# Output projection ordered by halves of x, with the transposes of x placed between products

## What is computed

```python
def rms_norm(x, g):
    y = x * rsqrt(mean(x * x) + NORM_EPS)
    return y * g
...
    x = x + concat(rms_norm(a, gain_a), rms_norm(b, gain_b), rms_norm(c, gain_c)) @ w_out
    x = x + relu(rms_norm(x, ln2_g) @ w_up) ** 2 @ w_down
```

## Time and profile before

| | us |
|---|---|
| median of 3 runs | 657.12 |
| lowest, highest | 655.36, 657.3 |
| the profiled execution, its own time | 657.18 |
| its span in the trace | 655.4 |
| TensorE busy | 618.9 |
| mean granted TensorE clock | 0.991 |

### The profile page before, as it was taken

One profiled execution on the slowest core, in us unless ns is written; L12 is line 12 of the kernel. 1 busy time (PEld: TensorE's weight loads), 2 busy tenths in 40 slices (PEclk: granted clock), 3 DMA queues, 4 the chain that ended last, 5 costly groups with the idle time before them and its releaser, 6 DMA issues.

```text
span 655.4 us, 11268 instructions
## 1 busy us (share of the span) xinstructions
PE 618.9 (94%) x4268; PEld 533.2 (81%) x4268; DVE 430.0 (66%) x796; ACT 361.6 (55%) x674; POOL 234.6 (36%) x407
## 2 busy tenths in 40 slices
PE   5999988998999999999999999799899999999995
PEld 4868865688998899889878787568798899899984
DVE  7599898476655696774575877846755545554553
ACT  5756588735546434443456657984545544444451
POOL 6899258515045999910004304771000000000001
PEclk9999998999999999999999999999899999999998
DMA  9584604156854557366638640314466566657631
GB/s 266 168 235 121 140 2 114 33 155 202 258 186 151 185 164 254 128 226 193 190 83 262 124 129 2 82 65 128 134 216 196 167 200 190 188 166 217 192 98 65
DMA packets 55440, 102.79 MB, mean 157 GB/s; under 512 B 12713, under 2 KB 18906, under 8 KB 55354
## 3 DMA queue, kind: packets, MB, share of 16 engines
q1 hardware_dynamic: 48986, 96.04, 48.2%
q0 software_dynamic: 1792, 4.07, 2.6%
q10 hardware_dynamic: 4608, 1.97, 1.1%
HBM read 99.69 MB, written 1.31 MB: 154 GB/s over the span
## 4 chain that ended last, share of the span: by engine, by line
PE 73%; DVE 15%; ACT 5%; issue 3%; POOL 2%; DMA 1%; SPq 0%; DVEq 0%; POOLq 0%; ACTq 0%
PE pb L1744 72%; DVE w_lo L1314 5%; DVE x L1242 2%; ACT tab_zone L1114 1%; ACT w_hi L871 1%; DVE dtmp L1235 1%; POOL dtmp L794 1%; DVE sc_zone L1638 1%; ACT ptmp L1127 1%; DMA raw<-in_w_in 1%; DVE dtmp L1514 1%; DVE top L1510 1%; PE pb L1871 1%; PE pb L2135 1%; DVE tab_zone L1235 1%
## 5 line engine op out<-in xcount | busy, mean ns | idle before, releaser
L1314 DVE TENSOR_TENSOR w_lo<-raw,w_hi 128x1024 fp32r<-128x1024 f32 (+2 forms) x176 | 223.6, 1286 | 139.5 <-ACT w_hi L871 138.6
L871 ACT ACTIVATE w_hi<-raw 128x1024 fp32r<-128x1024 f32 (+2 forms) x184 | 187.9, 1028 | 201.3 <-PE pb L1744 178.5
L1744 PE MATMUL pb<-h_hi,w_hi 128*128 128x256 f32 x512 | 146.1, 285 | 2.5 <-DVE h_lo L1242 1.8
L1744 PE MATMUL pb<-h_hi,w_lo 128*128 128x256 f32 x512 | 145.6, 284 | 0.0
L1744 PE MATMUL pb<-h_lo,w_hi 128*128 128x256 f32 x512 | 145.5, 284 | 0.0
L1744 PEld LDWEIGHTS pb<-h_hi,w_hi 128*128 128x128 f32 x512 | 98.9, 193 | 4.1 <-DVE w_lo L1314 3.0
L1744 PE MATMUL pb<-w_hi,z_hi 128*128 128x512 f32 x256 | 100.0, 390 | 0.4 <-DVE w_lo L1314 0.4
L1744 PE MATMUL pb<-w_hi,z_lo 128*128 128x512 f32 x256 | 99.9, 390 | 0.0
L1744 PE MATMUL pb<-w_lo,z_hi 128*128 128x512 f32 x256 | 99.7, 389 | 0.0
L1744 PEld LDWEIGHTS pb<-h_hi,w_lo 128*128 128x128 f32 x512 | 99.0, 193 | 0.4
L1744 PEld LDWEIGHTS pb<-h_lo,w_hi 128*128 128x128 f32 x512 | 98.9, 193 | 0.0
(11 more groups left out here) (309 smaller groups left out, 852.3 us busy)
## 6 DMA issues: line engine op xcount, KB each, us to landing
raw<-in_w_up SPq DMA_DIRECT2D x64, 512.0 KB, 3.7
raw<-in_w_down SPq DMA_DIRECT2D x64, 512.0 KB, 4.2
raw<-in_w_in SPq DMA_DIRECT2D x24, 512.0 KB, 4.9
raw<-in_w_out SPq DMA_DIRECT2D x8, 512.0 KB, 3.7
raw<-in_w_out SPq DMA_DIRECT2D x16, 256.0 KB, 4.1
raw<-in_w_in SPq DMA_DIRECT2D x8, 308.0 KB, 3.2
raw<-in_w_in SPq DMA_DIRECT2D x8, 280.0 KB, 3.0
x<-in_x ACTq DMA_DIRECT2D x4, 256.0 KB, 4.0
```

What stands on the lines that cost most here:

```text
L871: hi_made.by(act.activation(w_hi[:, n % RING, 0:width(n)], raw[:, n % RING, 0:width(n)], ACT.Copy))
L1314: lo_made.by(dve.tensor_tensor(w_lo[:, n % RING, 0:width(n)], raw[:, n % RING, 0:width(n)], w_hi[:, n % RING, 0:width(n)].bitcast(F32), AL ...
L1744: return pe.matmul(o, l, r, start=start, stop=stop, skip_group_check=True)
```

## The change

The order of the output projection becomes half 0 B, C, A, then half 1 B, C, A, on the same cycle of banks. Piece 23 is now half 0 A; pieces 24 to 27 are half 1 B, C, C, A. The two-load pieces (group C) are 21, 22, 25 and 26.

All six sums of squares are done at once behind piece 21 (`block_sums`), which waits for the squares of A too; there is one copy by ScalarE and one `rstd` of six columns.

For the MLP, the eight transposes of the first half of x stand ahead of piece 27 (`transpose_first`), and those of the second half behind the first piece of `w_up` (`transpose_second`), token tile by token tile, in banks 4, 7, 2, 3. The first `w_up` chunk takes its blocks in the order of `UP_ORDER`: 2, 3, 0, 1, 4 to 7. ScalarE makes `h_hi` of 2, 3, waits for piece 27 to be used, makes 0, 1, then `hi` of piece 31, then 4 to 7. VectorE makes `h_lo` of 2, 3 ahead of the last addition, the others behind it, and `lo` of piece 31 behind all of them.

Between the layers, half 1 of the last `w_down` product runs its first piece for both token tiles, then the other three for token tile 0 (`down_t0`), then the eight transposes of the first half of x, then the three pieces for token tile 1. The other eight transposes stand behind the next layer's first `w_in` piece. VectorE makes `lo` of that piece and the first two `h_lo` between its additions.

The diff, cut to its core:

```diff
-TWO_LOADS = (P_IN + 1, P_IN + 2, P_IN + 4, P_IN + 5)
+TWO_LOADS = (P_IN + 1, P_IN + 2, P_IN + 5, P_IN + 6)
...
-        OUT = [(0, 1, (1,), (0, 1)), (0, 2, (2, 3), (2, 3)), (1, 1, (1,), (5, 6)),
-               (1, 2, (2, 3), (0, 1)), (0, 0, (0,), (2, 3)), (1, 0, (0,), (5, 6))]
+        OUT = [(half, g, qs, banks) for half in range(2)
+               for g, qs, banks in ((1, (1,), (0, 1)), (2, (2, 3), (2, 3)), (0, (0,), (5, 6)))]
+        UP_ORDER = (2, 3, 0, 1, 4, 5, 6, 7)
...
-            bank = (0, 1, 2, 3)[k // 2] if stage == 0 else (4, 7, 5, 6)[k // 2]
+            bank = (0, 1, 2, 3)[k // 2] if stage == 0 else (4, 7, 2, 3)[k // 2]
...
-                rstd(L, 3, rg[:, 2:6], stat[:, 6:10], 1.0)
-                rstd(L, 4, rg[:, 0:2], stat[:, 4:6], 1.0)
-                rstd(L, 5, r2[:], stat[:, 10:12], D_MODEL)
+                rstd(L, 3, rg[:], stat[:, 4:10], 1.0)
+                rstd(L, 4, r2[:], stat[:, 10:12], D_MODEL)
...
-                    if L:
+                    if L and n < 2:
                         h_parts(L, 0, g1[:, L], (2 * n, 2 * n + 1))
+                if L:
+                    h_parts(L, 0, g1[:, L], range(4, KB))
...
                 for n in range(24, P_UP0 + 4):
-                    if n in (25, 27):
-                        i = (n - 25) // 2
-                        act.wait_ge(st_ps.sem, st_ps.at(L, i + 1))
-                        a, b = ((6, 10), (4, 6))[i]
-                        sq_sum.by(act.activation(stat[:, a:b], pb[7][:, a:b], ACT.Copy))
+                    if n == 25:
+                        act.wait_ge(st_ps.sem, st_ps.at(L, 1))
+                        sq_sum.by(act.activation(stat[:, 4:10], pb[7][:, 4:10], ACT.Copy))
+                    if n == P_UP0 + 3:
+                        h_parts(L, 2, g2[:, L], (2, 3))
+                        act.wait_ge(used.sem, used.at(L, P_UP0))
+                        h_parts(L, 2, g2[:, L], (0, 1))
                     hi(L, n)
-                h_parts(L, 2, g2[:, L])
+                h_parts(L, 2, g2[:, L], range(4, KB))
                 sums(L, 10, sq_sum.by)
...
-                    for n in ((25,), (26,), (27,), (28, 29), (30,), (31,))[s]:
+                    for n in ((25,), (26,), (27,), (28, 29), (30,), ())[s]:
                         lo(n)
-                h_rest(16, g2[:, L], lambda k: xT_rows(k, 2))
+                    if s == 4:
+                        h_rest(16, g2[:, L], lambda k: xT_rows(k, 2), UP_ORDER, 0, 2)
+                h_rest(16, g2[:, L], lambda k: xT_rows(k, 2), UP_ORDER, 2, 6)
+                lo(31)
...
                         for t in range(TT):
+                            if (half, t) == (1, 0):
+                                dve.wait_ge(down_t0.sem, down_t0.at(L, 1))
+                            if (half, t) == (1, 1):
+                                dve.wait_ge(used.sem, used.at(L, PIECES))
                             dst = x[:, t, half * 512:(half + 1) * 512]
                             x_new.by(stt(dst, pb[4 + 2 * t + half][:], r2[:, t:t + 1], dst, ALU.mult, ALU.add))
+                            if (half, t) == (0, 1):
+                                lo(0, 1)
+                            if (half, t) == (1, 0):
+                                h_rest(0, g1[:, L + 1], lambda k: xT_rows(k, 0), first=0, count=2, ahead=1)
...
+                def transpose_first(lyr, k_new, stage):
+                    pe.wait_ge(x_new.sem, x_new.at(lyr, k_new - 2))
+                    for k in range(4):
+                        for t in range(TT):
+                            m = x_turned(k, t, stage)
+                        if k % 2:
+                            xT_ps.by(m)
+                def transpose_second(k_new, stage):
+                    for t in range(TT):
+                        pe.wait_ge(x_new.sem, x_new.at(L, k_new - 1 + t))
+                        for k in range(4, KB):
+                            m = x_turned(k, t, stage)
+                            if k % 2 and t:
+                                xT_ps.by(m)
...
-                    pe.wait_ge(h_lo_made.sem, h_lo_made.at(L, (10, 14, 14, 14, 16, 16)[s]))
+                    pe.wait_ge(h_lo_made.sem, h_lo_made.at(L, (10, 14, 16, 16, 16, 16)[s]))
+                    if s == 5:
+                        transpose_first(L, 8, 2)
                     for q in qs:
                         out_piece(n, half, q, banks, q == qs[0], q == qs[-1])
                         n += 1
                         if n == P_IN + 2:
-                            pe.wait_ge(o_added.sem, o_added.at(L, 1))
-                            sums_of((1, 2))
-                        if n == P_IN + 4:
                             pe.wait_ge(o_added.sem, o_added.at(L, 2))
-                            pe.wait_ge(sq_sum.sem, sq_sum.at(L, 3))
-                            sums_of((0,))
-                transpose_x(12, 2)
+                            block_sums()
...
+                        if (c, q) == (0, 0):
+                            transpose_second(12, 2)
...
+                for t in range(TT):
+                    m = down_mm(CHUNKS - 1, 0, t, 1, False)
+                used.by(m)
+                for f in range(1, 4):
+                    m = down_mm(CHUNKS - 1, f, 0, 1, f == 3)
+                down_t0.by(m)
+                transpose_first(L + 1, 0, 0)
+                for f in range(1, 4):
+                    used.by(down_mm(CHUNKS - 1, f, 1, 1, f == 3))
```

More of the change, by code:

```diff
@@ L311, in trunk @@
         h_lo_made = sig("h_lo_made", 24)
-        sq_sum = sig("sq_sum", 5)
-        r_made = sig("r_made", 5)
+        sq_sum = sig("sq_sum", 4)
+        r_made = sig("r_made", 4)
         tile_sb = sig("tile_sb", len(TILES))
@@ L1309, in _, with lo, h_rest @@
             for L in range(DEPTH):
-                def lo(n):
-                    dve.wait_ge(hi_made.sem, hi_made.at(L, n + 1))
+                def lo(n, ahead=0):
+                    dve.wait_ge(hi_made.sem, hi_made.at(L + ahead, n + 1))
                     lo_made.by(dve.tensor_tensor(w_lo[:, n % RING, 0:width(n)], raw[:, n % RING, 0:width(n)],
                                                  w_hi[:, n % RING, 0:width(n)].bitcast(F32), ALU.subtract))
-                def h_rest(base, gains, src_of, order=range(KB), first=0, count=KB):
+                def h_rest(base, gains, src_of, order=range(KB), first=0, count=KB, ahead=0):
                     for i in range(first, first + count):
                         k = order[i]
-                        dve.wait_ge(h_hi_made.sem, h_hi_made.at(L, base + (i | 1) + 1))
+                        dve.wait_ge(h_hi_made.sem, h_hi_made.at(L + ahead, base + (i | 1) + 1))
                         h_lo_made.by(stt(h_lo[:, k, :], src_of(k), gains[:, k:k + 1],
@@ L1325, in _ @@
                 for n in range(4):
-                    if L:
+                    if L and n:
                         lo(n)
-                    h_rest(0, g1[:, L], lambda k: xT_rows(k, 0), first=2 * n, count=2)
+                    if L == 0 or n:
+                        h_rest(0, g1[:, L], lambda k: xT_rows(k, 0), first=2 * n, count=2)
                     if L == 0:
@@ L1762, in ready, with x_turned @@
                     pe.wait_ge(lo_made.sem, lo_made.at(L, n + 1))
-                def transpose_x(k_new, stage):
+                def x_turned(k, t, stage):
+                    return pe.transpose(xT_rows(k, stage)[:, t * PART:(t + 1) * PART],
+                                        x[:, t, k * PART:(k + 1) * PART], ident[:])
+                def transpose_first(lyr, k_new, stage):
[12 more added lines that the diff above has]
+                                xT_ps.by(m)
+                if L == 0:
                     for b in range(4):
[L1767 to L1770, removed]
+                        pe.wait_ge(x_loaded[b].sem, 16)
                         for k in (2 * b, 2 * b + 1):
                             for t in range(TT):
-                                m = pe.transpose(xT_rows(k, stage)[:, t * PART:(t + 1) * PART],
-                                                 x[:, t, k * PART:(k + 1) * PART], ident[:])
+                                m = x_turned(k, t, 0)
                         xT_ps.by(m)
-                        if L == 0 and stage == 0 and b == 0:
+                        if b == 0:
                             first_vectors()
-                transpose_x(0, 0)
                 def tile(i, after={}):
@@ L1785, in tile @@
                         pe.wait_ge(tile_sb.sem, tile_sb.at(L, i - 1))
+                    if L and i == 0:
+                        pe.wait_ge(x_new.sem, x_new.at(L, -1))
                     for q in range(4):
@@ L2163, in _, with block_sums @@
                         work()
-                def sums_of(groups):
-                    for g in groups:
+                def block_sums():
+                    for g in range(3):
                         for t in range(TT):
```

(27 more changed lines are left out.)

19 lines of the change are left out of this document (8 added, 11 removed).

## The result

The changed kernel takes 648.26 us in the median of 6 runs (646.77 to 650.41), the kernel before 657.03 (655.36 to 657.55, 6 runs beside them): a ratio of 0.9875, 95% interval 0.986 to 0.989. It is 1.2% faster. Two later comparisons gave 648.18 against 656.53 and 648.53 against 656.81. The profiled execution took 650.41 us, the longest of the six, so it is read stage by stage and not for its sum.

The account below looks back on a forecast made before the run. TensorE was taken to bound the kernel, with time to win only where it waits or runs slowly. 2 x 2.1 + 1.5 + 1.4 = 7.1 us off 657.18 gave 650.1 us, range 648.6 to 652.9.

Parts of the forecast that it names:

- What bounds: Whole kernel: TensorE, busy 94% of the span with 73% of the chain; time only where it stands still or runs slowly.
- The hand-overs: Output projection to MLP, each layer: moved transposes and the new order save TensorE 2.1 us, 4.2 us in all.
- Between the layers: Last w_down to next w_in: two transpose sets of 1.1 us replace the 3.67 us pause, gaining 1.5 us without waits.
- (a): Sums in layer 0's hand-over: A's squares end at 128.48, TensorE comes at 129.78, so 1.3 us of cover.
- (b): Behind the sums: ScalarE's copy 0.36 us later, six-column factors 1.4 us, VectorE adding from about 133.2 instead of 132.46.
- (d): Behind piece 26: VectorE's two additions, w_lo of piece 30 and two h_lo take 3.3 us, leaving 0.4 us of cover.
- The clock: Behind layer 1's hand-over: the dip to 1.2 GHz should go with the pause, gaining 1.4 us (bounds minus 1.4 to 1.4).
- 1: Clock dips anyway, behind a new transpose or in layer 1's attention: 651.5 us, 652.9 with one more dip; chance 0.25.
- 2: VectorE late in the hand-overs: 652.1 us if each waits 1 us, 654.3 if nothing is won there; chance 0.13.
- 3: Layer 0's load of piece 35, issued 5 us later, lands too late and makes the kernel slower; chance 0.02.
- 4: Reordering gains nothing, as a half of x is complete only after piece 27: 657 us; chance 0.02.

Follow-up runs that it names:

- e5: Changed kernel with four idle 128x512 VectorE copies between the two additions behind piece 26 and w_lo of piece 30, in both layers: 652.17 us, ratio 0.9931.
- e4: Kernel before with only the new output-projection order and the one sum of squares, all sixteen transposes still behind piece 27: 654.29 us, ratio 0.997.
- e3: Kernel before with only the part between the layers changed, both hand-overs to the MLP as before: 653.91 us, ratio 0.9967.
- e7: Kernel before with GpSimd's large table-preparing instructions for layer 1 spaced in pairs: 655.08 us, ratio 0.9976.
- e2: Changed kernel with the part between the layers put back, so only the hand-overs to the MLP changed: 650.28 us, ratio 0.9906.
- e1: Changed kernel again without any edit, for a second profile: 648.18 us, ratio 0.9874 to the kernel before.
- e6: Changed kernel with GpSimd's twelve large instructions for layer 1's tables in pairs behind separate MLP chunks, not six in a row: 647.68 us, ratio 0.9859.
- e8: Changed kernel with GpSimd's large instructions in pairs and h parts of blocks 2 and 3 ahead of hi and lo of piece 30: 647.04 us, ratio 0.985.
- e11: e8 repeated without edit, beside the unedited changed kernel on one chip: 647.13 us, ratio 0.9848 to the kernel before.
- e10: Changed kernel once more without edit, beside e9 and e11 on one chip: 648.53 us, ratio 0.9869 to the kernel before.
- e9: As e8, but GpSimd's large instructions in threes behind four chunks instead of pairs: 646.65 us, ratio 0.9856 to the kernel before.

## Why the prediction was right, and by how much it was off

- **What bounds.** Right. The gain is waiting of TensorE that is gone, and of the engines' shares of the chain only VectorE's changed (15 to 14%).
- **The hand-overs.** Forecast 2.1 us each, measured 2.5. The mis-sized term is the set of eight transposes, "I charge 1.1 us for a set of eight": it costs 0.79 us, 0.86 with the slower start of the next product, below the lower bound of 0.9. I had added the transposes' full length to a restart, where the last transpose overlaps what follows. Six sets make 1.4 us. About 0.2 went the other way: the merged sums take 1.26 us (130.02 to 131.28) where 1.17 was charged, and there is the wait of 0.05 us, in each layer.
- **Between the layers.** Forecast 1.5, measured 1.9 to 2.0, by the same term. The timetable held: VectorE's third addition, `h_lo` and the fourth addition came in the order given, 0.9 us earlier like the whole stage. The margin ahead of the `w_in` product, given as 0.8 us, is 0.5 (`h_lo` ends at 332.11, the product starts at 332.65), since the transposes cost less here too.
- **(a) and (b).** Right. The single sum makes no wait, VectorE's first addition starts at 133.47, and the forecast of 133.2 shifts to that with the 0.24 us that this execution was late at the sums.
- **(d), the tight place.** The chain's length was right (3.3 us forecast, 145.22 to 148.55 measured), the cover wasn't: since transposes cost less, TensorE is there 0.2 us sooner, and from the end of `h_lo` at 148.55 to the start of the product at 148.70 goes the rest. The changed kernel waits 0.05 us, and e5 shows that a further delay of 1.84 us is paid in full.
- **What the order is worth.** The prediction put all of the gain to the transposes' places. e4 shows that the order by itself gives 0.6 us in each hand-over, because VectorE is no longer behind when the last step ends; the places of the transposes give the rest of the 2.5.
- **The clock.** Forecast 1.4 us, and the dip behind the hand-over is indeed gone. The kernels with a pause of 4.27 us in their hand-overs (before, e3, e7) show one dip in their two hand-overs each, three in six; the pauses of 3.67 us (both hand-overs of e4, and between the layers in before, e2, e4, e7) none in six; in the changed kernel, e1, e2, e5, e6 and e8 to e11, which have no such pause, none falls behind a hand-over. Six against six is few, and e4's missing dips may be luck. By mean granted clock (its distance from 1, times the span) the kernel before loses 4.1 to 4.9 us in its runs to the lower level, the changed one 2.8 to 3.2. In the two comparisons that list the clocks of both (e1 and e10) it is 1.3 and 1.6 us less, one dip of 1.4. So the clock's term is borne out in size; what sets a dip off stays open. The rule of the Trainium skill that transposes don't count as busy for the clock the way matmuls do ("TensorE: Matmul & The Clock Gate", Part 4: PE-mode transpose) is neither shown nor refuted: a pause filled with sixteen of them has a dip or none, and 0.8 us of them between products never had one.
- **Rivals.** 1 fell (no dip anywhere near a hand-over). 2 fell, but with no margin left. 3 fell: the load of piece 35 was there before ScalarE could use it. 4 fell.
- **The sum.** 2 x 2.5 + 1.9 + 1.4 = 8.3 us; the three comparisons of medians give 8.8, 8.4 and 8.3. The forecast of 7.1 is 1.2 us below that sum, and the mis-sized transposes account for all of it (1.4, less the 0.2 above). The other 0.5 us of the first comparison has no row, and the later two don't show it. What the first profile showed on top, 1.4 us lost in layer 0's MLP and 0.24 us ahead of the sums, is why it fell on 650.41, near the forecast of 650.1 by chance.

## What to carry to other kernels

What an instruction costs an engine that pipelines is the distance to the next start, not its length; take it from rows where something follows, and where the trace has none, let the lower bound be the distance alone. A short detour (transposes) between long products costs its bare issue time only if what feeds it is done a step earlier, so order the steps by what the next stage needs first. And before adding the gains up, look who is just in time afterwards: here VectorE, whose next delay is paid in full (e5).

## What the runs showed of the hardware that was not expected

VectorE's 128x1024 subtraction from two SBUF tiles takes 1.22 us alone and 20.61 / 8 = 2.58 us in a row beside GpSimd's instructions of the same size, which take 2.9 us each, the last two of six 3.3 and 3.4 (e10). Six of those in a row can put VectorE so far behind that TensorE waits: in e10 the second six do (starts 0.69, 0.42 and 0.48 us apart), the first six don't. Three in a row don't (e9), nor do the four in e6. That the ring of four pieces is what sets the limit wasn't tested. The Trainium skill, "SBUF — State Buffer", Who interferes with whom, says that a VectorE instruction with two SBUF inputs contends with a GpSimd instruction that reads SBUF; by that rule, the trace agrees, and beside GpSimd's DMA issues the same instruction kept its 1.23 us (156.13 in the kernel before). How much of this reaches TensorE changes from one execution to the next: the same stretch takes 176.68 us in three profiles and 178.08 in the first, where e9 needs 175.31.
